# Product-key gather in half-token blocks, memory projections moved into the retrieval, convolution inputs first

## The reference, cut to what matters

```python
q = (xc @ w_q).reshape(C, 8, 2, 128)                 # 8 heads, two halves
s = einsum('chpd,hpnd->chpn', q, subkeys)            # 128 keys per half
sv, si = top_k(s, 16)
best, pos = top_k((sv[..., 0, :, None] + sv[..., 1, None, :]).reshape(C, 8, 256), 16)
ids = take_along_axis(si0 * 128 + si1, pos)          # 16 experts of 16384, per token and head
g = softmax(best)
a = gelu(einsum('cd,chkd->chk', xc, u[ids]))         # dot with a gathered row of u
y = einsum('chk,chkd->cd', g * a, v[ids])            # weighted sum of gathered rows of v
```

## Time and profile before

| | |
|---|---|
| median of 3 runs | 1860.47 us (1859.66 to 1860.87) |
| profiled execution | 1867.0 us, of which span 1865.0 us |
| busy PE / DVE / ACT / POOL | 1653.0 / 850.3 / 540.4 / 340.4 us |
| mean granted TensorE clock | 0.971 of full speed |
| read from HBM | 569.22 MB |
| first gather issued, last `dot` begun | 301.94 us, 969.71 us |
| second block's first projection, first `ho` matmul | 990.69 us, 1209.91 us |
| first expert matmul | 1388.09 us |

### The profile page before, as it was taken

The page is one execution under the profiler, slowest core; times in us unless marked ns, Lnnn a source line. Parts: engine busy times, 40 slices in busy tenths (PEclk is TensorE's granted clock), DMA queues, the critical chain, the costliest instruction groups (busy, mean ns, idle before and its releaser), DMA issues.

```text
span 1865.0 us, 19658 instructions
## 1 busy us (share of the span) xinstructions
PE 1653.0 (89%) x7276; PEld 995.6 (53%) x7276; DVE 850.3 (46%) x1893; ACT 540.4 (29%) x1316; POOL 340.4 (18%) x338
## 2 busy tenths in 40 slices
PE   8898998887878878788878999999979999999997
PEld 5486677543333222222237999887754444444442
DVE  1787728668886555554552677721231011010111
ACT  2213512244343443434342573101121111111111
POOL 0000002244444434344310048000000000000000
PEclk9999989999989999999999999999989999999999
DMA  8671026899999999999973444443339999999993
GB/s 355 229 289 47 1 90 252 343 364 427 426 427 427 427 427 427 427 427 427 427 303 126 163 151 179 157 151 135 136 118 431 427 429 429 430 429 431 429 403 129
DMA packets 65452, 571.28 MB, mean 306 GB/s; under 512 B 7520, under 2 KB 7776, under 8 KB 8416
## 3 DMA queue, kind: packets, MB, share of 16 engines
q1 hardware_dynamic: 25344, 281.13, 37.2%
q0 software_dynamic: 39312, 286.28, 37.0%
q10 hardware_dynamic: 720, 2.89, 0.4%
HBM read 569.22 MB, written 1.05 MB: 306 GB/s over the span
## 4 chain that ended last, share of the span: by engine, by line
PE 65%; DMA 16%; DVE 9%; ACT 6%; issue 3%; another core or an unknown queue 1%; SPq 0%; DVEq 0%; ACTq 0%
PE bank L1264 18%; DMA big<-in_peer_dram,big 14%; PE bank L1002 11%; PE bank L1098 6%; PE bank L875 3%; PE bank L1281 3%; PE bank L1256 3%; PE bank L1020 3%; DVE big L361 2%; PE bank L879 2%; ACT big L627 2%; PE bank L978 2%; PE bank L1172 1%; PE bank L1081 1%; PE bank L1078 1%
## 5 line engine op out<-in xcount | busy, mean ns | idle before, releaser
L1002 PE MATMUL bank<-big 128*128 128x512 f32 x1024 | 500.7, 626 | 123.2 <-ACT big L627 122.8
L1002 PEld LDWEIGHTS bank<-big 128*128 128x128 f32 x1024 | 185.1, 194 | 433.0 <-ACT big L627 271.4
L475 POOL DMA_INDIRECT big<-in_peer_dram,big x256 | 268.0, 1047 | 548.3 <-PE bank L1002 361.7
L1550 DVE SCALAR_TENSOR_TENSOR big<-big,misc 128x1024 f32<-128x1024 f32 x128 | 156.9, 1226 | 131.8 <-DMA big<-in_peer_dram,big 128.7
L1550 DVE SCALAR_TENSOR_TENSOR misc<-big,misc 128x1024 f32<-128x1024 f32 x128 | 156.8, 1225 | 114.8 <-DMA big<-in_peer_dram,big 114.6
L1264 PE MATMUL bank<-big 128*64 128x512 f32 x768 | 168.0, 592 | 1.3 <-ACT big L790 1.3
L1821 DVE TENSOR_TENSOR big<-big,bank 128x512 f32<-128x512 f32 x16 | 11.0, 687 | 297.8 <-PE bank L1264 297.8
L621 ACT ACTIVATE big<-big 128x1 f32<-128x1 f32 x256 | 51.5, 201 | 327.4 <-DVE big L1550 165.7
L1264 PE MATMUL bank<-big,misc 128*64 128x512 f32 x512 | 113.4, 594 | 9.7 <-ACT big L790 9.2
L1264 PEld LDWEIGHTS bank<-big 128*64 128x64 f32 x768 | 65.5, 137 | 100.1 <-issue 100.1
L627 ACT ACTIVATE big<-const,big 128x128 f32<-128x128 f32 x256 | 102.7, 401 | 11.0 <-PE bank L1002 2.7
(11 more groups left out here) (360 smaller groups left out, 2205.4 us busy)
## 6 DMA issues: line engine op xcount, KB each, us to landing
big<-in_moe_down_dram SPq DMA_DIRECT2D x32, 2048.0 KB, 11.4
big<-in_moe_up_dram SPq DMA_DIRECT2D x32, 2048.0 KB, 15.0
ring<-in_second_dram SPq DMA_DIRECT2D x44, 1024.0 KB, 4.8
big<-in_moe_gate_dram SPq DMA_DIRECT2D x16, 2048.0 KB, 12.0
ring<-in_moe_gate_dram SPq DMA_DIRECT2D x16, 2048.0 KB, 12.3
ring<-in_first_dram SPq DMA_DIRECT2D x29, 1024.0 KB, 5.2
misc<-in_mod_rest_dram POOLq DMA_DIRECT2D x16, 1024.0 KB, 5.4
big<-in_peer_dram,big POOLq DMA_INDIRECT x256, 19.9
```

Of the source, the lines that this page charges most:

```text
L475: pool.indirect_dma_start(out=gathered[b % GATHERS], out_offset=None, in_=t["peer"], in_offset=bass.IndirectOffsetOnAxis(ap=rows[:, b:b + ...
L1002: last = nc.tensor.matmul(bank[2 * tt + half][:], diag[:, b % DIAGS, :], gathered[b % GATHERS][:, a:a + 512], start=(h == 0 and k == 0), s ...
L1550: dve.scalar_tensor_tensor(products[b % 2], gathered[b % GATHERS][:, 0:UNIT], 1.0, x_rows[:, b // PTOP % TT, :], ALU.mult, ALU.mult, accum ...
```

## The change

There are six parts.
1. A block is now two picks by 64 tokens instead of one by 128. The row numbers and gates are turned to that layout by small matmuls (`turn_rows`, `turn_gate`, taken by DVE and ACT), the tokens' rows are laid out twice (`turn_x_pairs`), the diagonal is 128 x 64, and `add_pair` adds two blocks in four matmuls of 64 output rows each, the two token halves in the two halves of the array. PE frees buffers two at a time.
2. Gather buffers: 7 instead of 10 (their space holds the second copy of the tokens' rows and more). Diagonals: 8 instead of 4.
3. Queries, scores and top-k are made one head ahead only, the queries between the blocks; the scores keep 4 slots instead of 16.
4. Memory: loaded by SP among the first weights, its norm and the 16 units xk and xv are done between the blocks of the retrieval (two units in each of heads 1 to 6, four in head 7), with their 8 pairs in the first ring plan.
5. Second block: order ca, cg, f, q, i, then BETWEEN = g, gc, half of gr (16 units instead of 24, 0 to 3 for each level), the rest of gr later.
6. The 93 taps on DVE are spread: 24, 9 and 9 before the levels, 5 to 9 after each level; POOL's start as soon as ca and cg are there. The norm of the convolution comes before that of the recurrence.

```diff
-GATHERS = 10
+GATHERS = 7
 BLOCKS = 2 * PH * PTOP
-DIAGS = 4
+HALF = P // 2
+DIAGS = 8
 CONV_DVE = 3
 LEVELS = 7
+KV_PAIRS = [(), *[(7, 9)] * 6, (1, 3, 5, 7)]
+KV_TAKEN = [tuple(2 * p + 5 for p in pairs) for pairs in KV_PAIRS]
 
 
 W_IN_UNITS = [("dk", i) for i in range(4)] + [("gk", 0)] + [("dq", i) for i in range(4)] \
...
 def plan_first():
-    return [("mod", n) for n in range(16)] + W_IN_UNITS + [("out", n) for n in range(8)] + [("wq", n) for n in range(16)]
+    units = [("mod", n) for n in range(16)] + W_IN_UNITS + [("out", n) for n in range(8)]
+    for what, i in (("wq", 0), ("wq", 1), ("wq", 2), ("xk", 0), ("wq", 3), ("xk", 1), ("wq", 4), ("xk", 2), ("wq", 5), ("xk", 3),
+                    ("wq", 6), ("xv", 0), ("wq", 7), ("xv", 1), ("xv", 2), ("xv", 3)):
+        units += [(what, 2 * i), (what, 2 * i + 1)]
+    return units
 
 
 def plan_second():
     units = []
-    for what, a, b in (("f", 0, 4), ("q", 0, 4), ("i", 0, 4), ("gr", 0, 4), ("ca", 0, 4), ("cg", 0, 4), ("g", 0, 4), ("gc", 0, 8),
-                       ("gr", 4, 8), ("xk", 0, 8), ("xv", 0, 8), ("ho", 0, 4), ("co", 0, 4), ("mix", 0, 8), ("xq", 0, 8), ("xo", 0, 8)):
+    for what, a, b in (("ca", 0, 4), ("cg", 0, 4), ("f", 0, 4), ("q", 0, 4), ("i", 0, 4), ("g", 0, 4), ("gc", 0, 8), ("gr", 0, 8),
+                       ("ho", 0, 4), ("co", 0, 4), ("mix", 0, 8), ("xq", 0, 8), ("xo", 0, 8)):
         units += [(what, i) for i in range(a, b)]
     return units
 
@@ -68,7 +75,11 @@
 
 SECOND_ACT = [u for u in SECOND if u[0] not in ("co", "ho", "mix", "xo")]
...
+PARTS_AT = (0, 0, 3, 3, 3, 3, 2, 2)
+PARTS = [sum(PARTS_AT[:n]) for n in range(LEVELS + 2)]
+TAPS_EARLY = (24, 9, 9)
+TAPS_AT = (9, 9, 5, 5, 5, 5, 6, 7)
...
+                if n == (FIRST.index(("out", 6)) // 2) + RING:
+                    sp.dma_start(area(1024, 2048), t["memT"]).then_inc(S("mem_in"), 16)
...
-            sp.wait_ge(S("x2_ready"), base("x2_ready") + 1)
-            sp.dma_start(area(18048, 2048), t["memT"]).then_inc(S("mem_in"), 16)
...
+            kv = 0
+            for b in range(BLOCKS):
+                h, s = b // 32, b % 32
+                if h + 1 < PH:
+                    if s in (4, 9):
+                        take_query(2 * h + 2 + (4, 9).index(s))
+                    if s in (8, 12):
+                        take_scores(2 * h + 2 + (8, 12).index(s))
+                    if s == 19:
+                        gate_exp(h + 1)
+                    if s == 29:
+                        take_gate(h + 1)
+                if h == 0 and s == 14:
+                    act.wait_ge(S("mem_in"), 16)
+                    act.activation(sqm, memn, ACT.Square).then_inc(S("sqm_ready"), 1)
+                if h == 0 and s == 24:
+                    act.wait_ge(S("ssm_ready"), base("ssm_ready") + 1)
+                    act.activation(rsm, bank[5][:, 0:T], ACT.Sqrt, scale=1.0 / D, bias=eps).then_inc(S("stdm_ready"), 1)
+                if s in KV_TAKEN[h]:
+                    take_kv(kv)
+                    kv += 1
                 weigh(b)
                 if b == BLOCKS - 8:
                     take_y(0)
@@ -653,8 +704,6 @@
             for k in range(KT):
                 act.wait_ge(S("x2_ready"), base("x2_ready") + k + 1)
...
+            def add_pair(p):
+                h, tt, _ = block_of(2 * p)
+                j = p % (PTOP // 2)
+                pe.wait_ge(S("diag_ready"), 2 * p + 2)
                 for half in range(2):
                     a = UNIT + 512 * half
-                    last = nc.tensor.matmul(bank[2 * tt + half][:], diag[:, b % DIAGS, :], gathered[b % GATHERS][:, a:a + 512],
-                                            start=(h == 0 and k == 0), stop=(h == PH - 1 and k == PTOP - 1))
-                last.then_inc(S("block_done"), 1)
+                    for g in range(2):
+                        b = 2 * p + g
+                        last = nc.tensor.matmul(bank[2 * tt + half][HALF * g:HALF * (g + 1), :], diag[:, b % DIAGS, :],
+                                                gathered[b % GATHERS][:, a:a + 512], start=(h == 0 and j == 0), stop=(h == PH - 1 and j == PTOP // 2 - 1))
+                last.then_inc(S("block_done"), 2)
...
+            for p in range(BLOCKS // 2):
+                h, s = p // 16, p % 16
+                if h + 1 < PH:
+                    if s in (3, 5):
+                        key_scores(2 * h + 2 + (3, 5).index(s))
+                    if s in (0, 3):
+                        query(2 * h + 2 + (0, 3).index(s))
+                    if s == 10:
+                        turn_rows(h + 1)
+                    if s == 13:
+                        turn_gate(h + 1)
+                if h == 0 and s == 9:
+                    sum_mem()
+                if s in KV_PAIRS[h]:
+                    kv(u)
+                    u += 1
+                add_pair(p)
+                if p == BLOCKS // 2 - 2:
+                    pe.wait_ge(S("sc_ready"), 2 * PH)
+                    pe.wait_ge(S("kv_taken"), 16)
...
+                if lev < 2:
+                    project([("i", 2 * lev), ("i", 2 * lev + 1)], Hv)
...
+                    project_parts(range(PARTS[lev], PARTS[lev + 1]))
             pe.wait_ge(S("cross_ready"), 1)
             pe.wait_ge(S("level_taken"), LEVELS + 1)
...
+            def take_rows(h):
+                dve.wait_ge(S("rows_turned"), h + 1)
+                dve.tensor_copy(rows[:, 32 * h:32 * h + 32].rearrange("p (t j g) -> p t g j", t=TT, g=2),
+                                bank[7][:, 0:32].rearrange("p (t g j) -> p t g j", t=TT, g=2)).then_inc(S("rows_ready"), 1)
...
+                h, s = b // 32, b % 32
+                if h + 1 < PH:
+                    if s in (10, 14):
+                        top_keys(2 * h + 2 + (10, 14).index(s))
+                    if s == 16:
+                        top_pairs(h + 1)
+                    if s == 18:
+                        expert_rows(h + 1)
+                    if s == 22:
+                        normalise_gate(h + 1)
+                    if s == 24:
+                        take_rows(h + 1)
+                if h == 0 and s in (27, 29):
+                    mem_norm(range(0, 4) if s == 27 else range(4, 8))
                 dot(b)
 
...
+            some_taps(TAPS_EARLY[0])
+            dve.wait_ge(S("taken2"), SECOND_ACT.index(("f", 3)) + 1)
...
+            some_taps(TAPS_EARLY[1])
...
+            some_taps(TAPS_EARLY[2])
...
+                some_taps(TAPS_AT[lev])
```

More of the change, by code:

```diff
@@ L617, in weigh @@
             def weigh(b):
-                h, tt, k = b // 32, b // PTOP % TT, b % PTOP
                 c = slice(b, b + 1)
@@ L986, in _, with query @@
             subkeys = three(work[:, 0:2048], 16)
+            def query(n):
+                w = take()
+                if n >= 1:
+                    pe.wait_ge(S("qh_ready"), n)
+                for k in range(KT):
+                    if n == 0:
+                        pe.wait_ge(S("h2_ready"), k + 1)
+                    last = nc.tensor.matmul(bank[4][:, 0:T], w[:, k, :], Hv[:, k, :], start=(k == 0), stop=(k == KT - 1))
+                last.then_inc(S("first_unit_done"), 1)
             def key_scores(n):
@@ new lines, in turn_picks @@
+            def turn_picks(picks, at):
+                for tt in range(TT):
+                    of_tile = picks[:, tt, :].rearrange("p (j i) -> p i j", i=2)
+                    for g in range(2):
+                        a = at + tt * PTOP + g * PTOP // 2
+                        for i in range(2):
+                            last = nc.tensor.matmul(bank[7][HALF * i:HALF * (i + 1), a:a + PTOP // 2], ident[:, HALF * g:HALF * (g + 1)],
+                                                    of_tile[:, i, :], start=True, stop=True)
+                return last
@@ new lines, in add_pair, with sum_mem, kv @@
+                last.then_inc(S("block_done"), 2)
+            def sum_mem():
+                pe.wait_ge(S("sqm_ready"), base("sqm_ready") + 1)
+                for k in range(KT):
+                    last = nc.tensor.matmul(bank[5][:, 0:T], ones, sqm[:, k, :], start=(k == 0), stop=(k == KT - 1))
+                last.then_inc(S("ssm_ready"), 1)
+            def kv(u):
+                w = take()
+                if u == 0:
+                    pe.wait_ge(S("memn_ready"), 1)
+                else:
+                    pe.wait_ge(S("kv_taken"), u)
+                if u < 8:
+                    for k in range(KT):
+                        last = nc.tensor.matmul(bank[5][:, 0:T], w[:, k, :], memn[:, k, :], start=(k == 0), stop=(k == KT - 1))
+                else:
+                    for tt in range(TT):
+                        for k in range(KT):
+                            last = nc.tensor.matmul(bank[5][:, tt * P:(tt + 1) * P], memn[:, k, tt * P:(tt + 1) * P], w[:, k, :],
+                                                    start=(k == 0), stop=(k == KT - 1))
+                last.then_inc(S("first_unit_done"), 1)
```

361 lines of the change are left out of this document (177 added, 184 removed).

## The result

| | before | changed |
|---|---|---|
| median (5 runs each) | 1860.65 us | 1871.83 us (1867.34 to 1872.52) |
| ratio, 95% interval | | 1.0053 (1.0038 to 1.0068) |
| profiled execution, span | 1867.0, 1865.0 us | 1867.34, 1865.5 us |
| first gather | 301.94 us | 301.33 us |
| last `dot` | 969.71 us | 1014.25 us |

The forecast was 1862.5 us with a range of 1843 to 1885. The time lies in the range, 9.3 us above the forecast, and the kernel is slower, which had a chance of 0.45. The two profiled executions are 0.3 us apart: the gather stage (first gather to last `dot`) grew by 45.1 us, first projection to first `ho` shrank by 45.6.

A forecast was written before the change was run, and what follows sets the result against it. DMA engines bound the gather, PE then the convolution the second block, experts' weights the rest. +45 (gather) - 43 (second block) - 0.4 gave +2: 1869 us profiled, 1862.5 median, no measurable change; range 1843 to 1885.

The forecast's parts named there:

- First gather: Start of the gather stage: stays near 302 us; 0 taken, bounds -1 and +3.
- Bytes and holes: Gather stage: +8.8 us from more weight traffic, +36 from times with no gather in flight, 5.2 in each of 7 heads.
- Second block: First projection to `ho`: memory units leave PE, spread taps add waits; -43 us, bounds -53 and -34.
- the taps stand between the products and the next distances: Second block, levels 2 to 5: five DVE taps delay the following steps, 11.8 us a level instead of 10.3.
- Tail and the rest: After the gather's last block: 0.4 us less, since the memory's square no longer stands on ACT.
- Sum: Whole kernel: +45 - 43 - 0.4 = +2 us on the profiled execution, giving 1869.
- the medians lie 6.5 below it: Last step, from profiled execution to median: 1860.5 + 2 = 1862.5 us.
- The first: Gather stage: weights or gathers in flight fill the DMA gaps, 1 us a head; -27, 1833 us; chance 0.22.
- The second: Second block: taps on DVE set the pace, 13.5 us a level, gain only 31; +14, 1874 us; chance 0.12.
- The third: Gather stage: PE at the lower clock in all pairs and memory units, 9.4 us a head; +32, 1892; chance 0.13.
- The fourth: Gather stage: array halves do not run side by side, a pair costs 3.6 us; +13, 1876; chance 0.08.

The follow-up runs named there:

- rows20: Changed kernel with `expert_rows` before block 20 of a head instead of block 18; ratio 0.9841 to the kernel before, median 1834.84 us.
- taps_late: Changed kernel with `expert_rows` before block 20 and all 93 DVE taps behind the last level's copy; ratio 1.0018 to the kernel before, 1869.49 us.
- before_g7: Kernel before with 7 gather buffers instead of 10, nothing else; ratio 1.0023 to the kernel before, median 1870.36 us.
- taps_30: Changed kernel with `expert_rows` before block 20 and 30 instead of 42 taps before the first level; ratio 0.9869 to the kernel before, 1839.51 us.
- warm: Changed kernel with zero-adding matmuls behind the gather's pairs to keep TensorE busy; ratio 0.9975 to the kernel before, median 1860.88 us.
- kv_7_11: Changed kernel with the second memory unit of heads 1 to 6 moved from pair 9 to pair 11; ratio 1.0044 to the kernel before, 1873.61 us.
- warm20_light: Changed kernel with `expert_rows` before block 20 and four added matmuls behind most gather pairs; ratio 0.9883 to the kernel before, 1838.91 us.

## Why the prediction was right, and where it was off

**First gather**: 0 forecast, -0.6 measured. Right.

**Bytes and holes**: +8.8 and +36 forecast, +45.1 together measured. The stage holds the 11 + 4 pairs of weights of the forecast, and gathers land after 9.9 us (median; about 11 forecast). rows20 splits the sum: without the holes the stage is 12.9 longer than before, so the holes are 32 and the bytes with what is left 13. The forecast had seven holes; there are six. Heads 1 to 6 take 537.3 us, 31.6 more than their bytes (6 x 84.3), 5.3 each. So the count was one too high and some 4 us of other loss stood in no term; that the sum comes out within 0.3 us is luck. A hole's 5.3 fit the 5.2 taken, which was itself a choice between 1.0 and 9.4. Inside a hole some terms were off and partly cancelled. From `dot` 18 to the next gather the forecast had 2.2 + 3.3 + 0.4 + 3.45 + 1.74 + 0.27 = 11.4, measured 12.34: the second table load of `gate_exp` comes after `take_kv`, not before it (-1.4; the unit starts 4.49 after `dot` 18 instead of 5.9), and the unit, which begins at the lower clock, took 5.69 instead of 3.45 (+2.2). The pair took 1.94 instead of 1.74. The head above measured 89.7, forecast 84.3 + 5.2.

**Second block**: -43 forecast, -45.6 measured. Level 0's products start on PE 68.3 us after the first projection (66.3 forecast), PE having idled 10.2 us (8.5), but for another reason in part: 6.6 us of this idle time are there without any tap (taps_late); the taps add the rest. Levels 2 to 5 took 12.5, 10.5, 10.8 and 10.5 us, where I had 11.8 each and the kernel before takes 10.3. The term "the taps stand between the products and the next distances" was sized too high: 51 taps in the levels cost 3.9 us, since PE sets the pace there (8 products 1.8 and three split units 8.7 are 10.5). End of the convolution 150.2 after the first projection (151.3), `ho` 173.6 (176.3).

**Tail and the rest**: last `dot` to first projection -0.3 (-0.4 forecast). `ho` to the experts +1.8, where nothing was forecast; this stretch takes 178.3 to 181.2 in the other kernels with the same code, so it is spread.

**Sum**: +2 forecast for profiled executions, +0.3 measured. The step that failed is the last one, "the medians lie 6.5 below it". It holds for the kernel before (14 runs on the chips of the changed kernel's two comparisons took 1857.8 to 1861.3, its profiled execution 1867.0), not for the changed one, whose two profiled executions are its lowest runs. Carried over, it made 1862.5 out of a kernel that takes 1870 to 1872: no measurable change was forecast, and the kernel is 0.5% slower, clear of the noise. Where the 6.5 us of before's profiled execution lie stays open; before_g7, the same code but for the buffers, has 2.3 us less before the first gather and 3.1 less from first projection to `ho`, a hint and no more: it ran on another chip, and the first gather lies anywhere from 299.1 to 301.5 us in the kernels that change nothing ahead of it.

**The rivals.** The first (faster, holes closed, 1833) is what rows20 does: 0.9841 of 1860.65 is 1831. The change missed it by the place of one step. The second (DVE paces the levels) is true from 6 taps a level on (taps_30), not at 5. The third (every pair at the lower clock) is half true: the clock between 600 and 900 us fell to 0.78, from 0.99 in the earlier trace rows, and pairs take 1.94 or 3.68; but bringing it back in warm gave 5 of the 45 us by the traces and 14 by the ratios, and rows20 took 32 with the clock still at 0.84. The rule I had weighed for it (the Trainium skill, TensorE: Matmul & The Clock Gate, What's actually happening), that the throttled clock is the default and activity releases it, is borne out on the clock: PE's busy time in this stretch fell from 240.2 to 195.7 us of 300, and the clock with it. The fourth is out: a pair takes 1.94 us for eight records at the full clock, two blocks took 3.96 in the earlier trace rows.

## What to carry to other kernels

In a ring of buffers, add up all that can come late at one place: DVE's, ACT's and PE's steps between the same two blocks count together against the spare, and steps two or three blocks apart do not. Check the same sum for work that only moves there, and try the placement before giving up a design: here the change lost 0.5% with `expert_rows` before block 18 and won 1.6% with it before block 20. A difference under 0.5% between two kernels should not be read from one profiled execution of each: here these lay from 4.5 us below to 6.5 above the median of the same kernel.

## What the runs showed of the hardware

- A pair of blocks on PE after 4.8 to 8.4 us of idle time took 3.68 us, behind other PE work 1.94. So taking work away in front of a late matmul can also take away its clock: 1.7 of 3.4 us of gain remained (kv_7_11). The idle time just before does not settle it alone. In the changed kernel one pair took 3.68 us after 1.16 us of idle time, with another slow pair ahead of it, and one took 1.94 after 3.06. Level 0's products took 3.78 us after 10.23 of idle time, those of the later levels 1.95:
```profile
696.70 3.68 PE L1084 MATMUL bank<-big 128*64 128x512 f32 x8 [4.79 <-ACT big L663]
...
701.55 3.68 PE L1084 MATMUL bank<-big 128*64 128x512 f32 x8 [1.16 <-ACT big L663]
...
714.08 1.94 PE L1084 MATMUL bank<-big 128*64 128x512 f32 x8 [3.06 <-ACT big L663]
```
- Added matmuls raised the granted clock of this DMA-bound stage from 0.79 to 0.96 (warm) and from 0.84 to 0.94 (warm20_light). The ratio fell by 0.8% in the first and rose by 0.4% in the second.
- Code that is the same in several kernels took 680.7 to 685.5 us in the gather and 178.3 to 181.2 between `ho` and experts.
